# Index queries in two packed chunks of 512 columns, the index key beside two heads' queries, and the third chunk's first half unit in front of all

## The reference: what is computed

```
h    = RMSNorm(x)                                   # 256 x 2048
proj = h @ w_in                                     # w_in: 2048 x 13392
qa, ka, va, ga (1024 each), qi (1024), ki (64), wi (16), qb, kb, vb, gb (1024 each), ma, mb (2048 each) = split(proj)
qa, ka, qb, kb = rope(RMSNorm per head of 128 (..)) # 8 heads each
qi, ki = rope(..)                                   # 16 index heads of 64, one key
score  = sum over heads of relu(qi . ki) * wi       # causal
sel    = the 64 keys of the highest score for each query
oa     = softmax attention of qa over ka[sel], va[sel]
ob     = differential attention: softmax(map 0) - lam * softmax(map 1), over vb; RMSNorm
ya, yb = (oa * silu(ga)) @ w_o_a, (ob * silu(gb)) @ w_o_b
out    = x + (sigmoid(ma) * ya + sigmoid(mb) * yb) @ w_out
```

## Time and profile before

| | us |
|---|---|
| median of three runs | 776.13 |
| lowest, highest | 774.92, 776.16 |
| the profiled execution's own time | 776.79 |
| its span, first to last instruction | 775.0 |

### The profile page before, as it was taken

The page is one execution under the profiler, slowest core; times in us unless marked ns, Lnnn a source line. Parts: engine busy times, 40 slices in busy tenths (PEclk is TensorE's granted clock), DMA queues, the critical chain, the costliest instruction groups (busy, mean ns, idle before and its releaser), DMA issues.

```text
span 775.0 us, 10474 instructions
## 1 busy us (share of the span) xinstructions
PE 770.0 (99%) x3596; PEld 646.3 (83%) x3596; DVE 510.5 (66%) x718; ACT 423.6 (55%) x693; POOL 132.8 (17%) x225
## 2 busy tenths in 40 slices
PE   9999999999999999999999999999999999999998
PEld 8988888888888888888888888888888888888887
DVE  6679778778777655568656566566566567765553
...
GB/s 292 248 333 231 236 272 290 254 261 263 242 244 229 200 202 167 190 190 191 219 197 212 209 195 266 233 184 223 235 197 235 294 216 252 244 240 230 196 188 124
DMA packets 89579, 176.78 MB, mean 228 GB/s; under 512 B 7616, under 2 KB 15616, under 8 KB 89280
## 3 DMA queue, kind: packets, MB, share of 16 engines
...
...
## 4 chain that ended last, share of the span: by engine, by line
PE 93%; DMA 4%; DVE 1%; ACT 1%; SPq 1%; issue 0%
PE ps L718 30%; PE ps L719 30%; PE ps L720 29%; DMA raw<-in_w_in 4%; ACT hi L965 1%; DVE lo L1219 1%; PE ps L800 0%; PE ps L891 0%; PE ps L890 0%; PE ps L892 0%; SPq L444 0%; PE ps L788 0%; PE ps L801 0%; PE ps L802 0%; PE ps L803 0%
## 5 line engine op out<-in xcount | busy, mean ns | idle before, releaser
L1219 DVE TENSOR_TENSOR lo<-raw,hi 128x1024 fp32r<-128x1024 f32 (+2 forms) x279 | 333.8, 1202 | 237.7 <-ACT hi L965 236.7
L965 ACT ACTIVATE hi<-raw 128x1024 fp32r<-128x1024 f32 (+2 forms) x277 | 286.8, 1040 | 302.3 <-PE ps L720 265.7
L718 PE MATMUL ps<-hi,hT_hi 128*128 128x512 f32 (+1 forms) x912 | 353.0, 387 | 0.3 <-DVE lo L1219 0.3
L719 PE MATMUL ps<-lo,hT_hi 128*128 128x512 f32 (+1 forms) x912 | 352.6, 387 | 0.0
L720 PE MATMUL ps<-hi,hT_lo 128*128 128x512 f32 (+1 forms) x912 | 352.4, 386 | 0.0
L718 PEld LDWEIGHTS ps<-hi,hT_hi 128*128 128x128 f32 x912 | 171.2, 188 | 35.1 <-issue 0.5
L720 PEld LDWEIGHTS ps<-hi,hT_lo 128*128 128x128 f32 x912 | 171.2, 188 | 34.5
L719 PEld LDWEIGHTS ps<-lo,hT_hi 128*128 128x128 f32 x912 | 171.2, 188 | 33.5
L718 PE MATMUL ps<-hi,ogT_hi 128*128 128x512 f32 x128 | 49.8, 389 | 0.0
L719 PE MATMUL ps<-lo,ogT_hi 128*128 128x512 f32 x128 | 49.8, 389 | 0.0
L720 PE MATMUL ps<-hi,ogT_lo 128*128 128x512 f32 x128 | 49.8, 389 | 0.0
...
## 6 DMA issues: line engine op xcount, KB each, us to landing
...
```

The source lines that it names most:

```text
L718: mm(o, a_hi, w_hi[:, j], start=first and j == 0, stop=False)
L719: mm(o, a_hi, w_lo[:, j], start=False, stop=False)
L965: activation(hi[:, slot, :, 0:width], raw[:, slot, :, 0:width], ACT.Copy).then_inc(hi_ready, 1)
L1219: tt(lo[:, slot, :, 0:width], raw[:, slot, :, 0:width], hi[:, slot, :, 0:width].bitcast(F32), ALU.subtract).then_inc(lo_ready, 1)
```

## The change

It alters how the columns of the first input chunks are cut and when they are taken up.

- All 1024 index query columns go in chunks 0 and 1, 512 each, both packed.
- Chunk 2 holds key and head weights (80 columns) and two heads of qb (256), 336 columns, with 6 products for an inner tile. Its first unit stands first of all and its others among and behind those of chunks 0 and 1. Of the first three units the first halves of all three go ahead of the second halves (`rounded_part`, `low_part`).
- Chunks 3 and 4 hold three heads of qb each, 384 columns. Then kb, qa, ka, two chunks of 512 each. So there are nine chunks of heads, with the groups of heads that `QK_HEADS` names; a chunk of fewer heads uses its part of the staging tiles.
- They are taken up at the units in `QK_OUT`, rounded at those in `QK_COLUMNS`, and their remainders are made at those in `QK_LOW`. Squares are written to `roped` and wait for the turn of the chunk before (`qk_turned`), no longer for its landing in memory.
- The index takes two turns of four blocks, and the key one of its own.
- The loads of the small constants and of x's own rows stand at other units, warm-up is 7 products, and POOL clears the squares' sums once.

The core of the diff:

```diff
 X_CUTS = (0, 1, 2, 4, 6, 8, 10, 12, 14, 16)
 X_FRONT = KT + HD // 2
 EARLY = 3
-X_OWN_AFTER = ((3, 0), (3, 2), (3, 4), (3, 6))
+SINES_AT = 12
+X_OWN_AFTER = ((3, 2), (3, 4), (3, 6), (4, 0))
+ROWS_AFTER = ((2, 5), (2, 6), (2, 7), (3, 0), (3, 1), (3, 3), (3, 5), (3, 7), (4, 1))
 LO_STEP, LO_W = P + P // 2, P + P // 2 + P
 CK = 8
 RING = 4
-WARM_UP = 9
+WARM_UP = 7
 KIWI = IDX_DIM + IDX_HEADS
-IDX_W = (384, 384, 256 + KIWI)
-IDX_BLOCKS = tuple(w // P for w in IDX_W)
+
+
+FIRST_W = (512, 512, KIWI + 256, 384, 384)
+IDX_BLOCKS = (4, 4)
+KEY_GROUP = len(IDX_BLOCKS)
 A_W = A_HEADS * HD
...
 
-C_QK, C_V, C_G, C_M = 3, 11, 15, 19
+C_QK, C_V, C_G, C_M = 2, 11, 15, 19
+FIRST_COLS = (COL["qi"], COL["qi"] + 512, COL["kiwi"], COL["qb"] + 256, COL["qb"] + 640)
+assert COL["qb"] == COL["kiwi"] + KIWI
+
...
+QK_BLOCK = (24, 26, 28, 32, 36, 8, 12, 16, 20)
+QK_MAPS = (4, 5, 6, 4, 6, 0, 2, 0, 2)
+QK_GAINS = (2, 2, 2, 3, 3, 0, 0, 1, 1)
+QK_CHUNKS = len(QK_HEADS)
 C_O = 27
 U_O = C_O * CK
...
 
+
 PACKED = 2
-FIRST_UNITS = tuple((c, i) for i in range(CK) for c in range(PACKED))
-FIRST_END = 2 * CK - 1
-assert IDX_W[0] == IDX_W[1]
+THIRD_BEHIND = (0, 1, 2, 4, 6)
+FIRST_UNITS = ((2, 0), (0, 0), (1, 0))
+FIRST_UNITS += tuple(unit for i in range(1, CK) for unit in
+                     ((0, i), (1, i)) + (((2, THIRD_BEHIND.index(i)),) if i in THIRD_BEHIND else ()))
+FIRST_UNITS += tuple((2, i) for i in range(len(THIRD_BEHIND), CK))
+assert len(FIRST_UNITS) == 3 * CK
 
...
 def chunk_end(c):
-    return FIRST_END if isinstance(c, int) and c == 0 else c * CK + CK
+    return FIRST_UNITS.index((c, CK - 1)) + 1 if isinstance(c, int) and c < 3 else c * CK + CK
...
-    return IDX_W[c] if c < C_QK else CW
+    return FIRST_W[c] if c < len(FIRST_W) else CW
 
...
 
-INDEX_OUT = ((1, 7), (2, 4), (3, 3))
-INDEX_ROPE = (2 * CK, 3 * CK, 3 * CK + 4)
-
-X_SQUARES = ((4, 0), (4, 1))
-LATER = {C_QK: 3, C_QK + 1: 2}
-
-LATE = {C_QK: 2, C_QK + 1: 1}
+INDEX_OUT = (2 * CK + 4, 3 * CK + 2)
+INDEX_ROPE = ((2 * CK + 5, 2 * CK + 6, 3 * CK, 3 * CK + 1), (3 * CK + 3, 3 * CK + 5, 3 * CK + 6, 3 * CK + 7))
+INDEX_KEY, INDEX_TAKEN, LAM_AT = 5 * CK + 6, 8 * CK + 3, 4 * CK + 4
+
+X_SQUARES = ((4, 1), (4, 2))
+QK_OUT = (36, 42, 48, 54, 60, 66, 73, 80, 88)
+QK_COLUMNS = (46, 52, 58, 64, 70, 76, 83, 90, 96)
+QK_LOW = (48, 54, 60, 66, 72, 78, 85, 92, 96)
+assert QK_OUT[-1] == C_V * CK
...
 
-    return 6 if c == PACKED else 2 * ((c + 1) % 2)
+    return {0: 0, 1: 2, 2: 6, 3: 4, 4: 2, 6: 4}.get(c, 2 * ((c + 1) % 2)) if isinstance(c, int) else 2 * ((c + 1) % 2)
...
+            def load_small(c, i):
+                if (c, i) in ROWS_AFTER:
+                    to, row = rows[ROWS_AFTER.index((c, i))]
+                    sp.dma_start(to, row[0].partition_broadcast(P)).then_inc(consts_landed, 16)
+                if (c, i) in X_OWN_AFTER:
+                    load_x_own(X_OWN_AFTER.index((c, i)))
+
+            for j in range(2):
+                if j == 1:
+                    load_x(1)
+                for u in range(EARLY):
+                    load_first(u, j)
+            for u in range(EARLY, 3 * CK):
                 c, i = FIRST_UNITS[u]
                 if c == 0:
                     load_x(i + 1)
...
                 if u == EARLY + 1:
                     sp.dma_start(pos_i[:, :], positions).then_inc(phases_landed, 16)
-                if (c, i) in X_OWN_AFTER:
-                    load_x_own(X_OWN_AFTER.index((c, i)))
-
-            rows = [(gains[:, j], row) for j, row in enumerate((a_q_gain, a_k_gain, b_q_gain, b_k_gain))]
-            rows += [(lams[:, j], row) for j, row in enumerate((lambda_q1, lambda_k1, lambda_q2, lambda_k2))]
-            rows += [(sub_gain[:, :], b_subln_gain)]
-            for c, col in ((2, COL["qi"] + IDX_W[0] + IDX_W[1]),):
+                load_small(c, i)
+            for c in range(3, len(FIRST_W)):
...
-                load(i % RING, C_QK * CK + i, w_in, 2 * i, 0)
-                if (C_QK, i) in X_OWN_AFTER:
-                    load_x_own(X_OWN_AFTER.index((C_QK, i)))
-            with sp.Fori(1, 4) as n:
-                load_chunk(n + C_QK, n * CW)
+                    load(i % RING, c * CK + i, w_in, 2 * i, FIRST_COLS[c], FIRST_W[c])
+                    load_small(c, i)
+            with sp.Fori(0, 2) as n:
+                load_chunk(n + 5, n * CW + COL["kb"])
             with sp.Fori(0, 4) as n:
-                load_chunk(n + (C_QK + 4), n * CW + COL["qb"])
+                load_chunk(n + 7, n * CW)
...
                 pool.wait_ge(h_squares, n + 1)
                 root(r_h, ms_h, ss_h, HD, 8, NORM_EPS).then_inc(r_h_ready, 1)
                 if n == 2:
                     keep_index(2)
-                if 1 <= n <= C_QK:
+                if 1 <= n <= KEY_GROUP + 1:
                     t = n - 1
                     pool.wait_ge(index_kept[t], 16)
...
-            def early_unit(u):
+            def rounded_part(u, j):
 
                 c, unit_k = FIRST_UNITS[u]
-
-                bank = chunk_bank(c)
-                o_0, o_1 = ps[:, bank, 0:IDX_W[0]], ps[:, bank + 1, 0:IDX_W[0]]
-                for j in range(2):
-                    k, w_hi = 2 * unit_k + j, hi[:, u % RING, j, 0:IDX_W[0]]
-                    first = unit_k == 0 and j == 0
-                    pe.wait_ge(hi_first if j == 0 and u < EARLY else hi_ready, u + 1)
-                    pe.wait_ge(x_hi_first if j == 0 and u == 0 else split_hi, unit_k + 1)
-                    mm(o_1, hT_hi[:, k, P:S], w_hi, start=first, stop=False)
-                    pe.wait_ge(x_lo_first if j == 0 and u == 0 else split_lo, unit_k + 1)
-                    mm(o_1, lo_rows(k, 1), w_hi, start=False, stop=False)
-                    if j == 0 and u == 0:
+                k, bank, width = 2 * unit_k + j, chunk_bank(c), FIRST_W[c]
+                o_0, o_1 = ps[:, bank, 0:width], ps[:, bank + 1, 0:width]
+                w_hi = hi[:, u % RING, j, 0:width]
+                first = k == 0
+                pe.wait_ge(hi_first if j == 0 and u < EARLY else hi_ready, u + 1)
+                pe.wait_ge(x_hi_first if k == 0 else split_hi, unit_k + 1)
+                mm(o_1, hT_hi[:, k, P:S], w_hi, start=first, stop=False)
+                if c >= PACKED:
+                    mm(o_0, hT_hi[:, k, 0:P], w_hi, start=first, stop=False)
+                pe.wait_ge(x_lo_first if k == 0 else split_lo, unit_k + 1)
+                mm(o_1, lo_rows(k, 1), w_hi, start=False, stop=False)
+                if c >= PACKED:
+                    mm(o_0, lo_rows(k, 0), w_hi, start=False, stop=False)
+                else:
+                    if k == 0:
                         pe.wait_ge(x_again_first, 1)
                     mm(o_0, packed_rows(k), w_hi, start=first, stop=False)
-                for j in range(2):
-                    k, w_lo = 2 * unit_k + j, lo[:, u % RING, j, 0:IDX_W[0]]
-                    last = unit_k == CK - 1 and j == 1
-                    pe.wait_ge(lo_first if j == 0 and u == 0 else lo_ready, u + 1)
-                    mm(o_1, hT_hi[:, k, P:S], w_lo, start=False, stop=last)
-                    ins = mm(o_0, packed_rows(k), w_lo, start=False, stop=last)
-                ins.then_inc(unit_done, 1)
+
+            def low_part(u, j):
+
+                c, unit_k = FIRST_UNITS[u]
+                k, bank, width = 2 * unit_k + j, chunk_bank(c), FIRST_W[c]
+                o_0, o_1 = ps[:, bank, 0:width], ps[:, bank + 1, 0:width]
+                w_lo = lo[:, u % RING, j, 0:width]
+                last = k == KT - 1
+                pe.wait_ge(lo_first if j == 0 and u < EARLY else lo_ready, u + 1)
+                mm(o_1, hT_hi[:, k, P:S], w_lo, start=False, stop=last)
+                ins = mm(o_0, packed_rows(k) if c < PACKED else hT_hi[:, k, 0:P], w_lo, start=False, stop=last)
+                if j == 1:
+                    ins.then_inc(unit_done, 1)
 
             def w_in_unit(c, i, bank, width=CW):
 
-                if not isinstance(c, int) or c >= 2:
-                    if i == 0 and not (isinstance(c, int) and c == PACKED):
-                        pe.wait_ge(chunk_out, c - 1)
+                if not isinstance(c, int) or c > PACKED:
+                    if i == 0 and not (isinstance(c, int) and c == 3):
+
+                        pe.wait_ge(chunk_out, {4: 2, 5: 1, 6: 4}.get(c, c - 1) if isinstance(c, int) else c - 1)
                     unit(c * CK + i, i % RING, 2 * i, hT_hi, lo_rows, bank, i == 0, i == CK - 1, width)
 
             def warm_up(count):
@@ -760,23 +801,30 @@
 
             zeros = nc.const_aps.tensor(0.0, [P, P], F32)
             warm_up(WARM_UP)
-            for u in range(len(FIRST_UNITS)):
-                early_unit(u)
-            for c in range(2, C_QK + 2):
+            for j in range(2):
+                for u in range(EARLY):
+                    rounded_part(u, j)
+                    low_part(u, j)
+            for u in range(EARLY, 3 * CK):
+                for j in range(2):
+                    rounded_part(u, j)
```

(36 more changed lines are left out.)

324 lines of the change are left out of this document (162 added, 162 removed).

## The result

The changed kernel takes 780.03 us, median of 6 runs (778.79 to 782.18), the kernel before 775.87 in runs beside it (774.92 to 776.16). The ratio is 1.0060, with a 95% interval from 1.0045 to 1.0074: slower by 0.6%, where 0.5% faster was forecast. The profiled execution took 778.79 us, with a span of 777.0.

What follows compares the result with a forecast made beforehand. The prediction took PE, busy for 99% of the span, as the bound, its early waits carried by transfers. Terms -1.71, -0.64 and -1.76 on 776.79 gave 772.7, less 0.3 for the median: 772.4 us, range 771.0 to 775.1.

Steps and rivals of the forecast that it cites:

- The columns: Input projections: same 1024 products but 4096 fewer columns at 0.417 ns each, -1.71 us.
- The first units: Start of the kernel: the new order of half units cuts PE's waits from 1.59 to 0.95 us, -0.64.
- The wait for the fourth unit's weights: Start of the kernel: PE waits for late weights and their rounding, bounds 0.2 and 0.9, taken 0.6 us.
- The rest of the early stage: Early input units after the start: of 2.16 us of waits 0.4 stay, -1.76 us; bounds none gained and all.
- The cold clock: Rival: fewer warm-up products delay the clock's rise at the first products, 773.4 us; chance 0.10.
- The heads: Nine query and key chunks instead of eight, taken up every six units: cost nothing, bounds 0 and 1.5 us.
- a sign of being wrong: Waits of PE on splits between 110 and 190 us were to show the forecast wrong; forecast text says 110 to 200.
- the new wait: POOL's next root stands behind four transfers issued after the former chunk's low part, 4.1 us; DVE stands 0.2 to 0.8.
- the balance of DVE's 14.3 us against 16.3: DVE's work for one head chunk against the six-unit period, leaving 2.0 us of room.
- The lead of 3.2 us: Head chunks: DVE's splits run 3.2 us ahead of PE, which was to absorb DVE's waits.
- the six unit beat is too short: Rival: in head chunks, from a DVE wait of 2.0 us every period runs over, 778.4 us; severe case chance 0.05.
- The worst place: About unit 70, where the index's low parts fall: 17.7 us of DVE work in 16.3, leaving 1.8 of the lead.

Runs made afterwards that it cites:

- Experiment 8: Third chunk's half unit no longer leads the first units, against the changed kernel with two landing buffers: 776.93 us; against the one with six-and-a-half-unit beats: 786.02.
- experiment 2: Changed kernel with POOL's root for the next chunk's head norms worked out ahead of the four landing transfers: 778.23 us.
- experiment 7: With all edits: changed kernel plus second landing buffer, root before landings, later take-ups and low parts, seven units for each of the last four chunks: 774.12 us.

## Why the prediction was wrong

*The columns*, -1.71 us: right. The products lie on the same line, 0.2267 us at 512 columns and 0.23 from start to start above. The rule of the Trainium skill, page "TensorE: Matmul & The Clock Gate", section "Back-to-back issue gap", by which the term would have been an estimated 0.53 us, is not borne out by either trace.

*The first units*, -0.64: right in sign, too small. The wait for the fourth unit's weights, taken at 0.6, is 0.1, below the lower bound. Waits up to 12 us fall from 1.50 to 0.55, and the first product comes 0.12 earlier. In the other sixteen traces with this front these waits lie between 0.34 and 1.17, so the size varies from execution to execution. Experiment 8's 1.2 us for the place alone is no more than the difference of two medians.

*The rest of the early stage*, -1.76: right in sign, and at its outer bound. No wait is left between 12 and 100 us, so all of the 2.18 went. These two terms were -2.40 and are -3.1 to -3.25.

*The cold clock*, 773.4: did not come in the profiled execution, which has full speed from 5.68 us. It does in others: in that of experiment 2 five steps of 336 columns from 4.88 to 6.28 us are 0.28 apart in place of 0.153, 0.6 us in all, a third of what was taken. The kernel before was traced once, so whether its executions differ in the same way is open.

*The heads*, cost 0, bounds 0 and 1.5: **this is the step that failed**. It came to 6.45 us, in waits of PE for splits between 110 and 190 us, which the prediction had named as a sign of being wrong. The prediction named the new wait, its four steps and their 4.1 us, and the balance of DVE's 14.3 us against 16.3. Its mistake was to time the root once, from the end of ACT's rounding, with DVE on time, and to find 0.2 to 0.8 us. But the wait's beginning is DVE's own low part, and its end is DVE's next norm. Such a wait isn't added to a period now and then; the steps between norm and norm are a ring, and the ring must be summed up and set against 16.3 us. Of DVE's 14.3 us only one split of 1.15 lies beside the 4.8 us from low part to norm. The rest, with the low part at 0.6 in place of 1.3, is 12.4 and lies in a row with them: 17.2, and 17.15 measured. The lead of 3.2 us, which was to swallow the excess, was gone at once: DVE stood 3.91 us in front of the norm at 106.07, and PE's first waits follow at 111 us. This first wait is longer than the 0.2 to 0.8 us worked out for another reason, the home transfer of 5.68 us.

*The rival* "the six unit beat is too short" had the right place, the right mechanism and nearly the right sum (778.4), with a chance of 0.05. Its condition, a wait of 2.0 us or more, was met at four of the five norms between 100 and 180 us (3.91, 3.65, 1.83, 2.81, 3.66). It was priced by lateness of transfers and so given little. The first of the five norms is just that case, and it keeps its wait with two buffers (4.43 us); at the others it is the ring, which needs no late transfer.

*What the change is worth without it*: the three terms on the front side were right together. In the kernel of experiment 7 with all edits the profiled execution is 772.63 us, and the attention's first product starts at 245.4 us, where -1.71 for columns, -2.99 for early waits, -0.20 for the first product and +0.66 for what is left make 245.3 out of the 249.5 before. The quickest of 12 executions is what was traced; the median lies 1.3 us below that of the kernel before.

*The worst place* was put at unit 70, with the index's low parts. It is the largest single wait, 1.27 us at 185.98, but it is one fifth of the sum.
